# Re-ordering the opening of a two-sequence hybrid encoder layer on one core: memory rows, zero rows, masks, input turning and one output piece

## What is computed

```python
def encoder_layer(x, mem, ...):
    qa, ka, va, qb, kb, vb, qm = split(x @ w_in)          # three head groups
    mk, mv = split(mem @ w_mem_kv)
    oa = window_attention(qa, ka, va, sink)               # 8 heads, |t-s| <= 128, ALiBi
    ob = neighborhood_attention(qb, kb, vb, rpb)          # 4 heads, 8 x 16 window on an 8 x 64 grid
    om = memory_attention(qm, mk, mv)                     # 4 heads, 256 memory rows
    mixed = concat(group_rms(oa), group_rms(ob), group_rms(om))
    x = layer_norm(ALPHA * x + mixed @ w_out)
    return layer_norm(ALPHA * x + grouped_moe(x, ...))    # 16 experts, top 2 of one group of 4
```

## Time and profile before

| what | value |
|---|---|
| median of 3 runs | 1022.89 us (1021.92 to 1029.34) |
| the profiled execution | 1029.75 us |
| its span, first to last instruction | 1028.0 us |
| mean granted TensorE clock | 0.944 |
| busy TensorE matmul / weight load | 906.3 / 741.8 us |
| busy VectorE / ScalarE / GpSimd | 617.2 / 526.7 / 192.5 us |
| DMA | 183.54 MB, mean 179 GB/s |

### The profile page before, as it was taken

How to read it: one execution, slowest core, us unless ns; L and a number is a source line. 1 busy time by engine, 2 the same in 40 slices (tenths; PEclk the granted TensorE clock), 3 DMA queues, 4 the chain that set the end, 5 groups by cost and what they waited for, 6 DMA issues and landing times.

```text
span 1028.0 us, 15907 instructions
## 1 busy us (share of the span) xinstructions
PE 906.3 (88%) x4935; PEld 741.8 (72%) x4936; DVE 617.2 (60%) x1181; ACT 526.7 (51%) x982; POOL 192.5 (19%) x264
## 2 busy tenths in 40 slices
PE   5898999899989999989956899999999999999900
PEld 4766888677867788877725778888888888888800
DVE  4434643555744563556798889896645766446248
ACT  3343565542435555553453788785644846446212
POOL 4300002010000011000021335353222332222104
PEclk9998999899999999989967999999999999999965
DMA  8741114116322342213755999999777796772254
GB/s 264 139 66 42 41 42 132 54 54 213 112 74 82 119 169 70 95 41 97 304 201 185 364 331 375 373 394 369 224 211 238 254 333 207 215 232 44 33 184 164
DMA packets 94781, 183.54 MB, mean 179 GB/s; under 512 B 23825, under 2 KB 52736, under 8 KB 94736
## 3 DMA queue, kind: packets, MB, share of 16 engines
q1 hardware_dynamic: 80912, 139.48, 38.3%
q0 software_dynamic: 13824, 43.49, 16.6%
HBM read 159.33 MB, written 28.17 MB: 182 GB/s over the span
## 4 chain that ended last, share of the span: by engine, by line
PE 47%; DVE 10%; DMA 5%; issue 4%; ACT 3%; POOL 1%; DVEq 0%; POOLq 0%; ACTq 0%
PE O L1877 10%; PE C L1596 8%; PE C L1598 8%; PE C L1597 7%; DVE split_main L1507 3%; PE O L1777 3%; DMA acc_dram<-x_nat,idxs 2%; PE T L1830 2%; PE S L1631 2%; PE T L1752 2%; PE S L1837 1%; DMA x_nat<-x_dram,idxc 1%; PE T L1660 1%; DVE mixing L1581 1%; ACT split_main L1047 1%
## 5 line engine op out<-in xcount | busy, mean ns | idle before, releaser
L1507 DVE TENSOR_TENSOR split_main<-mixing,split_main 128x1024 fp32r<-128x1024 f32 x188 | 217.7, 1218 | 35.1 <-ACT split_main L1047 32.3
L1047 ACT CAST split_main<-mixing 128x1024 fp32r<-128x1024 f32 x188 | 186.4, 1049 | 17.2 <-PE C L1598 7.4
L1596 PE MATMUL C<-split_main,split_aux 128*128 128x512 f32 x368 | 143.3, 389 | 1.3 <-DVE split_aux L1513 1.3
L1598 PE MATMUL C<-split_main,split_aux 128*128 128x512 f32 x368 | 143.4, 390 | 0.0
L1597 PE MATMUL C<-split_main,split_aux 128*128 128x512 f32 x368 | 143.2, 389 | 0.0
L1596 PE MATMUL C<-split_main 128*128 128x512 f32 (+1 forms) x320 | 129.9, 406 | 9.7 <-DVE split_main L1349 6.3
L1877 PE MATMUL O<-split_main,split_aux 128*128 128x512 f32 x552 | 134.3, 399 | 0.0
L1597 PE MATMUL C<-split_main 128*128 128x512 f32 (+1 forms) x320 | 121.2, 379 | 0.0
L1598 PE MATMUL C<-split_main 128*128 128x512 f32 (+1 forms) x320 | 120.4, 376 | 0.0
L1877 PEld LDWEIGHTS O<-split_main,split_aux 128*128 128x128 f32 x552 | 101.4, 190 | 23.7 <-DVE split_aux L1528 4.5
L1596 PEld LDWEIGHTS C<-split_main 128*128 128x128 f32 x320 | 62.4, 195 | 28.9 <-issue 11.6
(11 more groups left out here) (303 smaller groups left out, 1425.4 us busy)
## 6 DMA issues: line engine op xcount, KB each, us to landing
mixing<-in_w_down SPq DMA_DIRECT2D x64, 512.0 KB, 7.3
mixing<-in_w_gate SPq DMA_DIRECT2D x64, 512.0 KB, 6.9
mixing<-in_w_up SPq DMA_DIRECT2D x64, 512.0 KB, 5.7
mixing<-in_w_in SPq DMA_DIRECT2D x20, 512.0 KB, 3.8
mixing<-in_w_out SPq DMA_DIRECT2D x16, 512.0 KB, 4.1
mixing<-in_w_mem_kv SPq DMA_DIRECT2D x8, 512.0 KB, 5.9
mixing<-in_w_in SPq DMA_DIRECT2D x16, 256.0 KB, 3.7
x_dram<-x_nat POOLq DMA_DIRECT2D x8, 512.0 KB, 2.9
```

The source lines that it names most:

```text
L1047: nc.scalar.copy(wu[0][:, w, :], raw[:, w, :]).then_inc(unit_hi, 1)
L1507: nc.vector.tensor_tensor(wu[1][:, w, :], raw[:, w, :], wu[0][:, w, :].bitcast(F32), ALU.subtract).then_inc(unit_lo, 1)
L1596: ins = nc.tensor.matmul(out_ap, st[0], mvg[0], start=first, stop=False)
L1598: ins = nc.tensor.matmul(out_ap, st[1], mvg[0], start=False, stop=last)
```

## The change

1. The memory rows are loaded in two loads of 512 KB with a semaphore each.
2. GpSimd makes the identity matrices and iotas first, and only then waits for the zero rows and issues the position bias. The zero row of `x1_dram` and its 512 KB write are gone (no gather reads it); that of `acc_dram` is written behind the loads of the spread bias, ahead of the small parameters.
3. In sequence 0 the first memory tile and `P` of chunk 0 go ahead of the second memory tile and `P` of chunk 1.
4. The masks move on VectorE from the start to behind both `P`, where the event of chunk 0's first quarter stands.
5. Sequence 0 has input tile 0 behind chunk 0, tiles 1 and 2 behind chunk 1, tile 3 behind chunk 2. Sequence 1 has tile 0 ahead of chunk 0, then tiles 1, 2, 3 behind chunks 0, 1, 2.
6. In both sequences tiles 0 and 1 of output piece 2 go ahead of the four `oB` units, tiles 2 and 3 stay behind.

```diff
+X_TILES = (((0,), (1, 2), (3,)), ((1,), (2,), (3,)))
@@ schedule
         if s == 0:
-            inputs(s, "m", range(MEM // P))
-            ev.append(("P", s, 0))
-            ev.append(("P", s, 1))
+            for t in range(MEM // P):
+                inputs(s, "m", (t,))
+                ev.append(("P", s, t))
+        else:
+            inputs(s, "x", (0,))
         for c in range(6):
             for q in range(4):
                 piece(s, c, q)
-            if c < NT:
-                inputs(s, "x", (c,))
+            if c < 3:
+                inputs(s, "x", X_TILES[s][c])
...
         wo(s, 0, 1, (2, 3), True)
+        wo(s, 0, 2, (0, 1))
         for n in range(NT):
             t_unit("oB", s, n)
         prepare(s, 3)
-        wo(s, 0, 2, (0, 1, 2, 3), True)
+        wo(s, 0, 2, (2, 3), True)
@@ SP
-            sp.dma_start(mem_nat, mem[0].rearrange("(t p) d -> p t d", p=P)).then_inc(mem_loaded[0], 16)
+            for t in range(MEM // P):
+                sp.dma_start(mem_nat[:, t, :], mem[0][t * P:(t + 1) * P, :]).then_inc((mem_loaded[0], mem_second)[t], 16)
@@ GpSimd
-            pool.wait_ge(setup_dve, 1)
-            pool.dma_start(o_sb[0:60, 0, 16:47], rpb.rearrange("h r c -> (h r) c")).then_inc(rpb_loaded, 16)
-            pool.dma_start(x1_dram[TT * P:(TT + 1) * P, :], o_sb[:, 3, :]).then_inc(pads_stored, 16)
-            pool.dma_start(acc_dram[TT * P:(TT + 1) * P, :], o_sb[:, 3, :]).then_inc(pads_stored, 16)
...
+            pool.wait_ge(setup_dve, 1)
+            pool.dma_start(o_sb[0:60, 0, 16:47], rpb.rearrange("h r c -> (h r) c")).then_inc(rpb_loaded, 16)
             pool.wait_ge(rpb_loaded, 16)
...
+            pool.dma_start(acc_dram[TT * P:(TT + 1) * P, :], o_sb[:, 3, :]).then_inc(pads_stored, 16)
             pool.dma_start(wr[:, :, :], w_router.rearrange("(k p) e -> p k e", p=P)).then_inc(small_loaded, 16)
@@ VectorE (the body of attention_masks is the old block, unchanged)
+                    if cu == 0 and q == 0:
+                        attention_masks()
...
                     if gi == 0:
-                        dve.wait_ge(pads_stored, 32)
+                        dve.wait_ge(pads_stored, 16)
@@ TensorE
-                        pe.wait_ge(mem_loaded[s], 16)
+                        pe.wait_ge(mem_second if (s, t) == (0, 1) else mem_loaded[s], 16)
```

More of the change, by code:

```diff
@@ L270, in bank @@
             return ctx.enter_context(nc.psum_tensor(name, [P, 512], F32))
-        x1_dram = nc.dram_tensor("x1_dram", ((TT + 1) * P, D), F32).ap()
+        x1_dram = nc.dram_tensor("x1_dram", (TT * P, D), F32).ap()
         acc_dram = nc.dram_tensor("acc_dram", ((TT + 1) * P, D), F32).ap()
@@ L404, in build_kernel @@
         mem_loaded = [sem(f"mem_loaded{s}") for s in range(NSEQ)]
+        mem_second = sem("mem_second")
         small_loaded = sem("small_loaded")
@@ L1269, in _ @@
                 nc.vector.memset(seed[:, i:i + 1], 0.0).then_inc(sm, v)
[L1270 to L1276, removed]
@@ L1277, in _ @@
-            link(nc.vector.tensor_scalar(d, o_sb[:, 0, 64:96], nv[:, 0:1], None, ALU.subtract))
-            gm = o_sb[:, 0, 128:224].rearrange("p (k c) -> p k c", k=3)
[L1279 to L1282, removed]
@@ L1283, in _, with attention_masks @@
-            link(nc.vector.tensor_tensor(gm[:, 1, :], gm[:, 1, :], o_sb[:, 0, 224:256], ALU.add))
-            link(nc.vector.tensor_scalar(gm[:, 2, 0:16], d[:, 0:16], 8.0, MASKED, ALU.is_lt, ALU.mult))
-            link(nc.vector.tensor_scalar(gm[:, 2, 16:32], d[:, 16:32], 23.0, MASKED, ALU.is_gt, ALU.mult))
+            gm = o_sb[:, 0, 128:224].rearrange("p (k c) -> p k c", k=3)
+            def attention_masks():
+                dve.wait_ge(setup_pool, 8)
+                link(nc.vector.scalar_tensor_tensor(dist, dist, -1.0, dist, ALU.mult, ALU.max))
+                link(nc.vector.tensor_scalar(mask, dist, float(WINDOW), MASKED, ALU.is_gt, ALU.mult))
+                link(nc.vector.tensor_scalar(scol[:, 1:2], scol[:, 0:1], 15, None, ALU.bitwise_and))
+                link(nc.vector.tensor_copy(nv[:, 0:1], scol[:, 1:2]))
+                d = o_sb[:, 0, 96:128]
+                link(nc.vector.tensor_scalar(d, o_sb[:, 0, 64:96], nv[:, 0:1], None, ALU.subtract))
+                link(nc.vector.tensor_scalar(gm[:, 0, 0:16], d[:, 0:16], -8.0, MASKED, ALU.is_lt, ALU.mult))
+                link(nc.vector.tensor_scalar(gm[:, 0, 16:32], d[:, 16:32], 7.0, MASKED, ALU.is_gt, ALU.mult))
+                link(nc.vector.tensor_scalar(gm[:, 1, :], d, 0.0, MASKED, ALU.is_lt, ALU.mult))
+                link(nc.vector.tensor_scalar(o_sb[:, 0, 224:256], d, 15.0, MASKED, ALU.is_gt, ALU.mult))
+                link(nc.vector.tensor_tensor(gm[:, 1, :], gm[:, 1, :], o_sb[:, 0, 224:256], ALU.add))
+                link(nc.vector.tensor_scalar(gm[:, 2, 0:16], d[:, 0:16], 8.0, MASKED, ALU.is_lt, ALU.mult))
+                link(nc.vector.tensor_scalar(gm[:, 2, 16:32], d[:, 16:32], 23.0, MASKED, ALU.is_gt, ALU.mult))
```

## The result

The changed kernel took 1021.60 us (median of 20 runs, 1016.84 to 1028.65), the kernel before 1027.14 in 20 runs beside it (1021.32 to 1035.06). The ratio is 0.9946, with a 95% interval of 0.9923 to 0.9968: about 5.5 us faster. The forecast was 4.2 us faster. The three runs of before that the forecast was carried over to lay low in the spread; with 20 of them the same -4.2 would give 1022.9.

A forecast was written before the change was run, and what follows sets the result against it. TensorE is busy for 88% of the span, so mostly only its idle time can be taken away. Terms -5.3 - 2.4 + 0.3 + 3.2 = -4.2 us take the median of 1022.89 to 1018.7; range 1012.9 to 1024.8.

The forecast's parts named there:

- The first opening: Start of sequence 0: chunk 4 starts at 32.5 instead of 37.81, 5.3 us gained; bounds 3.9 to 6.2.
- The chain up to chunk 0: First opening: memory rows, tile subtractions, then chunk 0's weight split; chunk 0 starts at 11.65 instead of 15.96, 4.3 us gained.
- which takes 20.45 - 15.96 = 4.5: First opening: chunk 0 was taken to last 4.5 us, with the masks, 3.1 us, beside it.
- chunk 2 at 24.4: First opening: chunk 2 starts at 24.4 against 25.47, leaving only 1.1 us of the 4.3 gained at chunk 0.
- the sign that the prediction named as wrong: Sequence 0: a granted clock under 1.00 in chunks 2 and 3 would show the prediction wrong.
- rival C: TensorE's clock falls in three new gaps, 2.8 us each: slower than before, +4.2 us, 1027.1; chance 0.11.
- the lower bound (3.9): First opening: least gain, 3.9 us, if the memory-row halves land together and chunk 0 is late.
- Masks gone: First opening: without masks ahead on VectorE, TensorE's start to the end of the first subtraction takes 1.12 us.
- rival B: First opening: both halves of the memory rows land at 6.3, chunk 0 starts at 12.6; -3.2 us overall, 1019.7; chance 0.14.
- The second opening: Start of sequence 1: 1.65 us lost at chunk 1, 4.1 gained ahead of chunk 4; -2.4 us, bounds 1.5 to 3.1.
- The output piece: Output stages: moving piece 2's tiles ahead of `oB` costs +0.3 us in sequence 0 and +3.2 us in sequence 1.
- rival A: Output stage, sequence 1: last piece not late, the burst catches up; 3.2 falls to 0.9, -6.5 us overall, 1016.4; chance 0.22.

## Why the prediction was right, and where not

**The first opening, -5.3 forecast, -2.94 in the profile.** The chain up to chunk 0 held: first units near 4.9 (4.28), second tile at 7.35 (6.78), chunk 0's landing at 8.0 to 8.4 (7.83), chunk 0 at 11.65 (11.49). Its last link is firm: in nine of the eleven profiles with the identities first, and in the one with the old head, ScalarE waited for chunk 0's weights and chunk 0 started 3.66 or 3.67 us after they landed. What the prediction lacked is the spread of that landing: 7.74 to 9.47 us, with chunk 0 from 11.40 to 13.13. That the changed kernel's profile met 8.0 and 11.65 so closely is in part luck: it is one of the earliest.

In the profile of after the step that failed is the time from chunk 0's start to chunk 4's, forecast as 20.85 us with the durations of before and measured as 23.38. Its first part is chunk 0, "which takes 20.45 - 15.96 = 4.5": the 4.49 of before was itself a mix of both clocks (its matmuls came 0.21 us apart, then 0.12), and after the change chunk 0 ran at the low clock to its end, 5.25 us. The tile behind it took 1.2 us instead of 0.8. Chunk 1 so ended at 21.05 instead of 20.05, and "chunk 2 at 24.4" became 25.93: behind the 2.41 us wait the clock was low, and tile 2 took 1.60 us to chunk 2's start, against 1.01 in the run with the split ahead. From chunk 2 to chunk 4 the forecast was 8.1 us. That run, at the high clock, took exactly that (25.44 to 33.54); the changed kernel's profile took 8.94. So in this profile the 2.4 us that are missing are all clock, and the sign that the prediction named as wrong, a granted clock under 1.00 in chunk 2, is there (second line; the first belongs to the last section):

```profile
12.00:16.00 4.00, 4.00 (x21) 4.00 (x20) 3.11 (x13) 0.00 (x0) 0.88 (x2) 1.00 1.11 343
...
24.00:28.00 4.00, 3.67 (x18) 3.67 (x19) 2.26 (x4) 1.20 (x2) 0.00 (x0) 0.57 0.49 135
```

These are windows of after: length, busy time and count of TensorE, its weight loads, VectorE, ScalarE and GpSimd, the granted clock, DMA share and GB/s. It was one fall of rival C's three, and it cost 1.4 us (0.59 ahead of chunk 2, 0.84 behind), half of the 2.8 that the rival gave it. The other two gaps kept their clock (granted 1.00 from 262 to 268 and from 498 to 503 us). The clock is not the whole account, though. In three other runs with the same opening (the output piece back, the split ahead, sequence 1's tiles as before) chunk 2 kept the high clock, and chunk 4 started at 34.05, 33.54 and 33.91. There chunk 0 was late, at 13.13, 12.57 and 12.58, because its weights landed late, and from its start to chunk 4's it took 20.92, 20.97 and 21.33 us, near the forecast. With 34.87 the mean is 34.1. The old opening has 37.81, and 37.96 in the run with the output piece alone, so about 3.8 us is the fairer reading, just under the lower bound (3.9) that the prediction gave.

**The masks.** "Masks gone" was not needed. Once GpSimd's iotas come at 3.6 us, the masks at the start cost 0.54 us on the second units and nothing at chunk 0. What freed VectorE was the order of GpSimd: it brought the iotas from 7.2 to 3.6 us, and the prediction named it only for the identities.

**The halves landing together (rival B).** Refuted: 4.28 against 6.13 with one load. But nothing of the 1.85 us shows at chunk 0, whose own load set it; the prediction's chain had that load in it, and still counted 0.9 us there for the split ("3.4 if the two halves land together").

**The second opening, -2.4.** Right: -2.57, undone to 20.42 us by putting the order back. Chunk 1, forecast 1.65 us late, came 1.60 late against the opening (268.20 - 262.16 = 6.04, before 270.85 - 266.41 = 4.44); 1.12 of it is the new wait.

**The output piece.** Right in both sequences: +0.20 for +0.3, +2.63 for +3.2. The link by which it acts was the one named: the low part of piece 3, SP's down loads, a burst of loads that takes 20.5 to 20.8 us whenever it starts, ScalarE's wait, the last piece. It waited 1.69 us; without that wait it would have been 0.94 us late, the 0.9 that rival A gave. The term was 0.6 too large because the down loads went out 2.88 us later, not 3.2, and the burst was 0.25 us shorter. Rival A falls: the queue does not catch up.

**The sum.** -4.2 forecast, -5.5 measured. The interval, -7.9 to -3.3 us, holds the forecast. The profiles differ by 7.1 us, of which 4 lie in the two stretches that were long in the one of before. The four steps of the change make -2.7 in the profiles, and -3.5 with the fairer reading of the first opening. So some 2 us of the median's 5.5 are placed by no run, and that -4.2 came so near to it is in part luck: the opening was taken too large, the output piece's loss too.

## What to carry to other kernels

Where several loads share a queue at the start, find the one whose landing has a fixed distance to the first large matmul, over several profiles; putting another load first only moved the wait to the one that was now last (chunk 0 at 11.79). An independent piece of matmul work moved into a place without idle time is not free if a DMA issue hangs on what it pushes back: follow the release of the buffer slot to the loads behind it. To take away a wait for a subtraction, put the tile ahead of the other work of the engine that subtracts, inside a chunk, instead of adding it to the chunk before (19.5 us from chunk 0 to chunk 4 against 20.9 to 23.4, in one profile).

## What was not expected of the hardware

**The same wait, two outcomes.** The wait of 2.41 us behind chunk 1 stands in six profiles. In three the granted clock from 24 to 28 was 0.57, 0.62 and 0.57, in three 1.00. The Trainium skill, TensorE: Matmul & The Clock Gate, section What's actually happening, says that the gate judges activity over a window that runs free of the kernel's start, so that the number of slow matmuls differs from run to run. Two outcomes of one wait fit that; no run here shows that it is the reason. Over 65 executions of the kernel before, the time falls by 9.8 us for each 0.01 of mean granted clock (correlation -0.86), and over the 20 of the changed kernel by 8.1 (-0.84): most of the scatter of 12 to 14 us goes with the clock. Which of the two moves the other was not tried.

**One GpSimd instruction of 7 us.** GpSimd, kernel before, first expert:

```profile
578.83 7.01 POOL L978 TENSOR_TENSOR idxs<-idx,izero 128x1 int32<-128x1 int32 x1 [7.74 <-ACT x_nat L1207]
```

and TensorE, 28 us later:

```profile
607.38 0.50 PE L1830 MATMUL T<-ident,x_nat 128*128 128x128 f32 x2 [1.99 <-DMA x_nat<-x_dram,idxc]
```

The same instruction took 0.39 us in the profile of after. The gather that follows came late, and TensorE waited 1.99 us for it, and from the first expert matmul to the end it was 474.9 us against 472.6. Of the other twelve profiles one has it again (6.93 us, TensorE waiting 2.18), the run with tile 3 inside chunk 3. What causes it was not tried. It is not the change, since it stands in a profile of the kernel before.
